# Alternating two sums of small matmuls between the upper and lower 64 rows of the TensorE array

## The reference, cut to what matters

```python
kc_blk = (partial_rope(kc, cos, sin)[:, tok] + cmp_pos[0]).reshape(Bsz, n_cmp, CMP_LEN * d)
k_cmp = rms_norm(kc_blk @ cmp_w[0], k_norm_w[0])
v_cmp = (vc[:, tok] + cmp_pos[1]).reshape(Bsz, n_cmp, CMP_LEN * d) @ cmp_w[1]
```

## Time and profile before

| What | us |
|---|---|
| median of 3 runs | 3252.81 |
| lowest and highest run | 3252.35, 3255.76 |
| span of the profiled execution (first to last instruction) | 3251.6 |
| busy: PE, DVE, POOL, ACT | 2586.7, 2429.2, 2099.9, 799.4 |

### The profile page before, as it was taken

How to read it: one execution, slowest core, us unless ns; L and a number is a source line. 1 busy time by engine, 2 the same in 40 slices (tenths; PEclk the granted TensorE clock), 3 DMA queues, 4 the chain that set the end, 5 groups by cost and what they waited for, 6 DMA issues and landing times. The chain is left out here.

```text
span 3251.6 us, 30183 instructions
## 1 busy us (share of the span) xinstructions
PE 2586.7 (80%) x8860; PEld 1539.4 (47%) x8860; DVE 2429.2 (75%) x5632; ACT 799.4 (25%) x1853; POOL 2099.9 (65%) x2059
## 2 busy tenths in 40 slices
PE   8878677898897687888788687899898687666666
PEld 7767333666465342565455342566566342222222
DVE  2323998768778998768868998768777999666664
ACT  2521122234321122123421122233331122111111
POOL 0000677657676777657776777756776777777775
PEclk9859899999899799898899899999899889888889
DMA  5103899999999999999999999999999999999999
GB/s 189 53 14 139 343 409 409 411 410 375 366 364 410 370 396 410 411 412 387 400 392 410 391 403 409 410 411 393 369 345 411 398 378 409 409 409 410 409 410 354
DMA packets 311313, 1187.51 MB, mean 365 GB/s; under 512 B 34544, under 2 KB 34544, under 8 KB 298352
## 3 DMA queue, kind: packets, MB, share of 16 engines
q0 software_dynamic: 294912, 1073.87, 84.1%
q1 hardware_dynamic: 16240, 111.72, 8.7%
HBM read 1183.36 MB, written 2.10 MB: 365 GB/s over the span
## 5 line engine op out<-in xcount | busy, mean ns | idle before, releaser
L755 PE MATMUL acc<-v_rows,diag 128*128 128x512 f32 x2728 | 1440.6, 664 | 472.4 <-DMA v_rows<-expert_v,idx 388.8
L1417 DVE CUSTOM_DVE_ANT_0 u_rows<-u_rows,h 128x1024 f32<-128x1024 f32 x1024 | 1231.8, 1217 | 400.3 <-DMA u_rows<-expert_u,idx 398.7
L1478 POOL DMA_INDIRECT u_rows<-expert_u,idx x1024 | 1056.2, 1031 | 637.7 <-DVE idx L1382 276.7
L1491 POOL DMA_INDIRECT v_rows<-expert_v,idx x1024 | 1041.9, 1017 | 453.2 <-issue 258.4
L755 PEld LDWEIGHTS acc<-v_rows,diag 128*128 128x128 f32 x2728 | 528.5, 209 | 1196.5 <-issue 1016.2
L1435 DVE SCALAR_TENSOR_TENSOR X<-v_rows,wgt,X 128x1024 f32<-128x1024 f32 x342 | 439.2, 1284 | 48.2 <-DMA v_rows<-expert_v,idx 42.6
L1033 ACT ACTIVATE diag<-consts,wgt 128x128 f32<-128x128 f32 x682 | 255.2, 395 | 741.7 <-PE acc L755 561.9
L465 PE MATMUL bank<-HT,w_ring 128*128 128x256 f32 x1792 | 411.7, 386 | 2.2 <-DVE HT L1041 2.2
L465 PEld LDWEIGHTS bank<-HT,w_ring 128*128 128x128 f32 x1792 | 349.0, 195 | 91.4 <-issue 44.6
L474 PE MATMUL bank<-w_ring,HT 128*128 128x256 f32 (+1 forms) x1280 | 279.3, 375 | 7.0 <-ACT arena L766 7.0
L766 ACT ACTIVATE arena<-bank 128x256 f32<-128x256 f32 (+4 forms) x304 | 112.9, 382 | 670.5 <-PE bank L465 254.0
(11 more groups left out here) (185 smaller groups left out, 2027.2 us busy)
## 6 DMA issues: line engine op xcount, KB each, us to landing
w_ring<-weights SPq DMA_DIRECT2D x100, 1024.0 KB, 8.0
u_rows<-expert_u,idx POOLq DMA_INDIRECT x1024, 11.8
v_rows<-expert_v,idx POOLq DMA_INDIRECT x1024, 11.9
X<-in_x SPq DMA_DIRECT2D x2, 1024.0 KB, 6.4
out<-X SPq DMA_DIRECT2D x4, 512.0 KB, 6.4
n2w_wide<-parameters SPq DMA_DIRECT2D x2, 512.0 KB, 8.3
params<-parameters SPq DMA_DIRECT2D x2, 412.0 KB, 7.6
consts<-constants SPq DMA_DIRECT2D x1, 749.5 KB, 6.3
```

The costliest lines, as they stand in the source:

```text
L755: last = T.matmul(acc[:, at_h], diag[:, i % DIAG_RING], v_rows[:, t % V_RING, at_h], start=(at_t == 0), stop=(t == max(q for q in range(t ...
L1417: made(V.tensor_tensor_reduce(out=rows_u, in0=rows_u, in1=h2[:], scale=1.0, scalar=0.0, op0=ALU.mult, op1=ALU.add, accum_out=dots[:, b % 2 ...
L1478: pool.indirect_dma_start(out=u_rows[:, s % U_RING, :], out_offset=None, in_=u_dram, in_offset=bass.IndirectOffsetOnAxis(ap=idx[:, n % 2, ...
L1491: pool.indirect_dma_start(out=v_rows[:, t % V_RING, :], out_offset=None, in_=v_dram, in_offset=bass.IndirectOffsetOnAxis(ap=idx[:, t // PE ...
```

## The change

Before, the 32 matmuls of `ck` were issued one behind the other and then the 32 of `cv`. Now both banks are taken at `cm0`, and each of the four phases issues, for 8 places j, the matmul of `ck` and the matmul of `cv` in turn. The number of matmuls, their operands and the number in each phase (16) are the same. The last matmuls of both sums now stand at the end of `cm3`.

```diff
                     if i == 0:
                         wait_slot(S_CMP)
                         pe.wait_ge(sig("cmp_z"), nth(n, "cmp_z", 1))
-                    name, lo = (("ck", HD), ("cv", 0))[i // 2]
-                    if i % 2 == 0:
-                        out = take(pe, f"{n}.{name}", "cr")
-                    for j in range(16 * (i % 2), 16 * (i % 2) + 16):
-                        last = T.matmul(out[0:64, 0:CMP_PAD], weights[lo:lo + 64, j, :], cmp_z[lo:lo + 64, j, :],
-                                        start=(j == 0), stop=(j == CMP_LEN - 1))
-                    if i % 2:
-                        full(last, f"{n}.{name}")
+                        sums = [(name, lo, take(pe, f"{n}.{name}", "cr")) for name, lo in (("ck", HD), ("cv", 0))]
+                    for j in range(8 * i, 8 * i + 8):
+                        for name, lo, out in sums:
+                            last = T.matmul(out[0:64, 0:CMP_PAD], weights[lo:lo + 64, j, :], cmp_z[lo:lo + 64, j, :],
+                                            start=(j == 0), stop=(j == CMP_LEN - 1))
+                            if j == CMP_LEN - 1:
+                                full(last, f"{n}.{name}")
```

## The result

The changed kernel takes 3228.07 us (median of 4 runs, 3226.95 to 3232.66) against 3252.58 us (4 runs): a ratio of 0.9928, 95% interval 0.9915 to 0.9941. That is 0.72% faster, some 23 us, with 19 to 28 in the interval. One run of the kernel with blocks of four (4309.00 us) and one of the kernel before beside it (4139.55 us) ran at a granted clock of 0.695 and 0.552 and are left out of all medians and ratios here. The forecast was 3245.3 us in a range of 3240.5 to 3251: the direction was right, the size was a third of what came, and the time lies outside the range.

The account below looks back on a forecast made before the run. The prediction took step 0's PE, DVE and ACT chain as the bound up to about 270 us, then the gathers. 5.5 + 2.0 = 7.5 us off 3251.6 gives 3244.1, plus 1.2 for the median: 3245.3 us, range 3240.5 to 3251.

Parts of the forecast that it names:

- The pace of a record: L637 burst, step 0: alternating halves cuts a record's start from 107 to 59 ns, 128 records from 13.43 to 7.8 us.
- the seam: Where `cv` follows `ck` in the old L637 burst: different array halves overlap, 10 records in 0.85 us, 62 ns each.
- the last 32: Last 32 L637 records in steps 1 to 3, after the `acc` sum: already at 59 ns, gain nothing.
- The copies: DVE copies behind both sums in step 0: two copies of 0.28 us now stand in a row, adding 0.16 us.
- Step 0 net: Step 0: 5.6 us gained in the L637 burst, less 0.16 us for the DVE copies, net 5.5 us.
- the clock: Clock rise in step 0 may shift against the work: plus or minus 2 us, nothing in the mean.
- Both banks at `cm0`, the `w_ring` load: Step 0: asking for `cv`'s bank 64 records earlier costs nothing; SP's next load moves ahead and no one waits for it.
- Steps 1 to 3: Later bursts: 96 records shrink to 5.9 us, DVE waits some 4, but the total gains only 2.0 us, bounds 0 to 3.5.
- A: L637 burst: only half of the overlap comes, 83 ns a record, 10.8 us in step 0, total 3249.4 us; chance 0.13.
- B: L637 burst: each change from upper to lower half drains the array, 0.29 us each, total 3316 us; chance 0.05.
- C: No overlap to speak of in the L637 burst, or gathers give back step 0's gain; total 3253.0 us; chance 0.08.
- The sum: Whole kernel: 5.5 + 2.0 = 7.5 us off a span of 3251.6, median run 3245.3 us, 0.23% faster.

Follow-up runs that it names:

- kernel with blocks of four: Changed kernel, but `ck` and `cv` alternate in blocks of four matmuls (8 records) instead of one; 3231.84 us, ratio 0.9931 to the kernel before.
- run with DVE padded: Changed kernel plus 4 extra DVE products of 128x1024, results thrown away, at phase `t2` of steps 1 to 3; 3245.91 us, ratio 0.9975 to the kernel before.
- kernel with step 0 alone: Changed kernel with `ck` and `cv` alternating only in step 0, old order in steps 1 to 3; 3246.33 us, ratio 0.9980 to the kernel before.
- control: Kernel before with both PSUM banks taken at `cm0` but the old matmul order kept; 3253.29 us, ratio 1.0001 to the kernel before.
- run with steps 1 to 3 alone: Changed kernel with `ck` and `cv` alternating only in steps 1 to 3, old order in step 0; 3234.44 us, ratio 0.9935 to the kernel before.

## Why the prediction was right or wrong

*The pace of a record.* Right. 107 ns came from one half of the array, and the seam's overlap carried over the burst. The size was a little off: I took 59 ns as what can be issued, and 53 ns came, so 7.04 us instead of 7.8. The 59 was no issue rate. In the run with DVE padded the last 32 records of step 1 at the full clock took 1.12 us:

```profile
808.13 1.12 PE L636 MATMUL bank<-arena,w_ring 64*64 64x32 f32 x32
```

A start came every (1.12 - 0.22) / 31 = 29 ns. So 59 was one half's pace at full clock, and it halves too. The forecast that the last 32 gain nothing was wrong for that reason, by 0.6 us in step 1.

*The copies.* Right: 0.17 us more between the burst's end and the transposes (160.43 - 159.80 = 0.63, before 0.46), forecast 0.16.

*Step 0 net.* Right. Forecast 5.5, measured 13.43 - 7.04 - 0.17 = 6.2 us; the kernel with step 0 alone gave 6.5, and from the burst to the first `u` gather six profiles on each side differ by 5.5 us. The first gather of the profiled execution came 8.2 us earlier; 2.1 us of that is chance, since the burst begins that much earlier though nothing ahead of it changed. It begins at 152.52 us in a kernel in the old order, too. I had allowed 2 us for the clock; what makes this spread isn't shown.

*Both banks at `cm0`, the `w_ring` load.* Right: for the banks the control shows no difference (ratio 1.0001), and among PE's waits of the changed kernel up to 270 us there is none for a load.

*Steps 1 to 3.* This is the step that failed: "Here the gain is nearly used up", with 2.0 us and an upper bound of 3.5. The term is 14 to 16 us by the profiles and 21 (17 to 25) by the run with steps 1 to 3 alone. The lengths of the bursts and DVE's wait were about right (5.9 forecast and 5.33 measured, "some 4" and 3.57). What I did wrong was to price them by POOL's waits in the 20 us behind the burst and to call a gather part with a full DMA share insensitive. The stretch from 1020 to 2300 us, from which the share of 1.01 comes, holds nothing of the stretch of step 1 and only the first 27 us of that of step 3; over those stretches the share was 0.97. The long waits of POOL began nearly 70 us behind the burst, and PE, which in that time had no wait for a `v` tile, didn't make up for it. Much of the price stood there, in waits for PE that add up to 16.2 us before and 8.1 after.

*The rivals.* A (half of the overlap) falls with 53 ns. B (a drain at each change of halves) falls with it. C (no overlap, or step 0's gain given back) falls with both the burst and the 6.5 us of the kernel with step 0 alone. None of the rivals was the case that came: the gain of the later steps was in no case's list, so the range could not hold it.

*The sum.* 6.2 + 14.3 to 16.0 is 20.5 to 22.2 us, inside the measured 19 to 28. What stays open is the remainder of 1 to 3 us, which the profiles' own spread covers; how the gain of steps 1 to 3 divides between PE's shorter burst and DVE's shorter wait; and why the three stretches react as much to a shift by one slot (17 us) as to 5 us of work a step.

## What to carry to other kernels

Small matmuls on up to 64 rows that are bound by the start of one after the other can be run on both halves of the array, with results in different banks, at half the time; blocks of four on one half were nearly as good as strict alternation. Two sums in one bank weren't tried.

Before pricing time saved on an engine that serves a ring, look along its waits for the first place where it catches up with what feeds it. If there is none, look on to where the ring runs out. Here the first long wait stood nearly 70 us behind the saving, and a window of 20 us missed it.

Where a chain passes from engine to engine, the wait names only the last of them; a pad on each in turn tells which of them time can be lost on.

## What the runs showed of the hardware

Two streams of these float32 matmuls (64 x 64 against 64 x 32) on the two halves of the array keep their own pace, 107 ns each at the low clock and 59 ns at the full one, and together start every 53 and 29 ns. On one half and two banks they start every 107 ns. The granted clock was 0.50 through the burst of step 0 in both kernels, with 128 records in 13.43 us and in 7.04. And PE starts records of the other half ahead of those that still wait: with blocks of eight records on one half the burst took 7.83 us, 0.8 more than with strict alternation.
